# Experts' gate and up projections by Strassen's seven products on 64-column tiles, down blocks spread behind the products

## The reference, cut to what matters

```
D_MODEL = 1024
...
N_EXPERTS = 16
...
D_EXPERT = 2816
...
    xe = h[bidx, idx]
    hid = jax.nn.silu(jnp.einsum('becd,edf->becf', xe, e_gate)) * jnp.einsum('becd,edf->becf', xe, e_up)
    ye = jnp.einsum('becf,efd->becd', hid, e_down) * gate[..., None].astype(h.dtype)
    return jnp.zeros_like(h).at[bidx, idx].add(ye)
```

## Time and profile before

| what | us |
|---|---|
| time, median of 3 runs | 3615.91 (3611.45 to 3624.05) |
| span of the profiled execution | 3612.2 |
| first transpose of the experts' stage | 1489.76 |
| first gate matmul | 1494.90 |
| last down matmul ends, about | 3594.96 |

### The profile page before, as it was taken

The page is one execution under the profiler, slowest core; times in us unless marked ns, Lnnn a source line. Parts: engine busy times, 40 slices in busy tenths (PEclk is TensorE's granted clock), DMA queues, the critical chain, the costliest instruction groups (busy, mean ns, idle before and its releaser), DMA issues.

```text
span 3612.2 us, 83473 instructions
## 1 busy us (share of the span) xinstructions
PE 3408.1 (94%) x37698; PEld 2976.7 (82%) x37698; DVE 1102.5 (31%) x2770; ACT 735.5 (20%) x1815; POOL 385.0 (11%) x536
## 2 busy tenths in 40 slices
PE   7989898898999997499999999999999999999998
PEld 3575767667455544499999999999999999999998
DVE  4566666575344444411111111111111111111113
ACT  3435344343244433000000000000000000000002
POOL 0141514233211000000000000000000100000001
PEclk9999999999999998799999999999999999999999
DMA  8200000000311122697777778787778878777775
GB/s 353 71 5 9 18 10 17 5 20 5 102 32 26 43 77 93 226 362 264 281 269 275 268 274 275 264 288 258 272 276 280 275 267 283 263 281 269 274 264 185
DMA packets 500080, 666.46 MB, mean 185 GB/s; under 512 B 31598, under 2 KB 438406, under 8 KB 496654
## 3 DMA queue, kind: packets, MB, share of 16 engines
q1 hardware_dynamic: 494030, 641.74, 50.5%
q0 software_dynamic: 5520, 19.34, 2.0%
q10 hardware_dynamic: 176, 0.05, 0.0%
HBM read 631.68 MB, written 28.30 MB: 183 GB/s over the span
## 4 chain that ended last, share of the span: by engine, by line
PE 58%; SPq 1%; DMA 0%; DVE 0%; ACT 0%; issue 0%; DVEq 0%
PE banks L2465 38%; PE banks L2477 19%; PE banks L2488 0%; PE banks L2423 0%; DMA e_wd<-in_e_down 0%; SPq L2335 0%; SPq L2339 0%; SPq L2336 0%; SPq L2334 0%; ACT e_wd L2558 0%; PE banks L2447 0%; DVE e_ye L2632 0%; DVE e_wu L2718 0%; DVE e_wu L2661 0%; DVE e_xe L2707 0%
## 5 line engine op out<-in xcount | busy, mean ns | idle before, releaser
L2465 PE MATMUL banks<-e_xT,e_wg 128*128 128x144 f32 x5632 | 747.9, 287 | 1.9 <-DVE e_xT L2598 1.6
L2477 PE MATMUL banks<-e_hid,e_wd 128*128 128x144 f32 x5632 | 748.1, 287 | 0.0
L2465 PE MATMUL banks<-e_xT,e_wu 128*128 128x144 f32 x5632 | 747.6, 287 | 0.0
L2465 PEld LDWEIGHTS banks<-e_xT,e_wg 128*128 128x128 f32 x5632 | 713.8, 191 | 2.4 <-DMA e_wd<-in_e_down 2.3
L2465 PEld LDWEIGHTS banks<-e_xT,e_wu 128*128 128x128 f32 x5632 | 713.8, 191 | 0.0
L2477 PEld LDWEIGHTS banks<-e_hid,e_wd 128*128 128x128 f32 x5632 | 711.1, 191 | 0.0
L2608 DVE TENSOR_TENSOR e_tm<-banks,e_sg 128x144 f32<-128x144 f32 x352 | 108.3, 308 | 1790.3 <-ACT e_sg L2544 1790.3
L2544 ACT ACTIVATE e_sg<-banks 128x144 f32<-128x144 f32 x352 | 102.1, 290 | 1937.6 <-PE banks L2465 1937.6
L606 PE MATMUL banks<-hT_x,wblk 128*128 128x512 f32 (+1 forms) x624 | 212.7, 496 | 0.0
L606 PEld LDWEIGHTS banks<-hT_x,wblk 128*128 128x128 f32 x624 | 102.8, 192 | 100.1 <-issue 98.5
L1398 DVE TENSOR_TENSOR r_TW<-r_TW,banks 128x256 f32<-128x256 f32 (+1 forms) x360 | 129.3, 392 | 78.3 <-PE banks L830 74.1
(11 more groups left out here) (383 smaller groups left out, 3572.0 us busy)
## 6 DMA issues: line engine op xcount, KB each, us to landing
e_wg<-in_e_gate SPq DMA_DIRECT2D x176, 1024.0 KB, 5.2
e_wu<-in_e_up SPq DMA_DIRECT2D x176, 1024.0 KB, 7.5
e_wd<-in_e_down SPq DMA_DIRECT2D x176, 1024.0 KB, 10.2
h_wmod<-in_w_mod SPq DMA_DIRECT2D x24, 1024.0 KB, 15.2
wblk<-in_w_in SPq DMA_DIRECT2D x22, 512.0 KB, 21.5
h_x<-in_x_sample SPq DMA_DIRECT2D x8, 512.0 KB, 6.8
wo<-in_w_out SPq DMA_DIRECT2D x2, 2048.0 KB, 12.0
scratch_ffn<-hT_x SPq DMA_DIRECT2D x8, 512.0 KB, 5.2
```

The lines of the kernel that those rows point to most:

```text
L2465: last = nc.tensor.matmul(bank[6 + b % 2][:, j * TOK:(j + 1) * TOK], w[s][:, k, f], xT[e % 2][:, k, :], start=(k == 0), stop=(k == KD - 1))
L2477: last = nc.tensor.matmul(bank[k // PER_BANK][:, c:c + TOK], wd[s][:, b % DUO, k * P:(k + 1) * P], hid[:, b % 2, :], start=(b == 0 and k % ...
```

## The change

**What is computed.** For a duo, gate (and likewise up) is a product of a 256 x 1024 by a 1024 x 144 matrix. It is cut in two by two: hidden units in halves of 128 (columns 0 to 127 and 128 to 255 of a tile), the contraction in halves of 512, tokens in halves of 72 (`HT`). Instead of eight products of these halves seven are formed, of sums of them, and the four results are mixed from the seven. `mats(n)` is 2 for every duo: gate and up both go this way.

**PE.** `product(n, g, q)` is one of the seven for gate (g = 0) or up (g = 1): four pieces of 128 contraction rows, and for each two matmuls, on weight columns 0 to 63 and 64 to 127 (`CS`), to PSUM partitions 0 to 63 and 64 to 127, with 72 tokens streaming. All seven results of one matrix lie in one bank (4 or 6 for gate, 5 or 7 for up). `down` is cut into units of one 128-column output piece, two matmuls of 64 weight columns with 144 tokens, 16 units a duo; `due` gives each unit its step, one or two behind each of the 14 products of a duo, two duos later, and none for some seven steps at an expert's end. The transposes (`turned`) are now matmuls of 64 columns against the identity, four blocks in a row behind the product with q = 3, all through bank 3.

**DVE.** Per duo: four sums of weight halves of 128x1024 elements (L2710, L2715, L2720, L2725), two duos ahead; the mixing of four operations (L2743 to L2750); two multiplications of 128x288 (L2754, L2762). Per expert: four token sums of 128x288 (L2691 to L2696).

**ACT and SP.** ACT copies the first product out (`first_out`) and takes one sigmoid of 288 per duo. Gate and up of a duo share a tile of 2 MB, four of them (`WG`), free when the duo's products are done (`gu_ps`); `wd` keeps six. In the last expert the norm is done four tokens' tiles at a time, behind duos 8 to 10.

```diff
+    def mats(n):
+        return 2 if True else 1
+    def due(i):
+        e, r = divmod(i, ND * UNITS)
+        return STEPS * (ND * e + 2) + r * (STEPS * (ND - 1) + 8) / (ND * UNITS)
...
+        wgu = [sb(f"wgu{i}", [P, 2, KD, DUO * P]) for i in range(WG)]
+        wd = [sb(f"wd{i}", [P, DUO, D]) for i in range(WD)]
+        wsum = [sb(f"wsum{i}", [P, 3, 2, HALF, P]) for i in range(2)]
...
-        SQUARES = {14: (0, 1), 15: (2, 3), 16: (4, 5), 17: (6, 7)}
-        SCALES = {18: (0, 1), 19: (2, 3), 20: (4, 5), 21: (6, 7)}
+        SQUARES = {8: (0, 1, 2, 3), 9: (4, 5, 6, 7)}
+        SCALES = {9: (0, 1, 2, 3), 10: (4, 5, 6, 7)}
...
+                for n in range(N):
+                    e, j = divmod(n, ND)
+                    f = slice(j * DUO * P, (j + 1) * DUO * P)
+                    if n >= WG:
+                        sp.wait_ge(gu_ps, n - WG + 1)
+                    sp.dma_start(wgu[n % WG][:, 0, :, :], gv[:, e, :, f]).then_inc(g_in[n % WG], 16)
+                    sp.dma_start(wgu[n % WG][:, 1, :, :], uv[:, e, :, f]).then_inc(g_in[n % WG], 16)
+                    if n >= WD:
+                        sp.wait_ge(used, n - WD + 1)
+                    sp.dma_start(wd[n % WD][:, :, :], dv[:, e, j * DUO:(j + 1) * DUO, :]).then_inc(d_in[n % WD], 16)
...
+                    for c in CS:
+                        if c.start < n:
+                            c = slice(c.start, min(c.stop, n))
+                            last = nc.tensor.matmul(bank[b][c, out], src[:, c], K.ident[:, :], start=True, stop=True)
+                    return last
...
+                    s = n % WG
+                    x, xs, ws, w = xT[n // ND % 2], xsum[n // ND % 2], wsum[n % 2], wgu[s][:, g, :, :]
+                    k1, k2, f1, f2 = slice(0, HALF), slice(HALF, KD), slice(0, P), slice(P, 2 * P)
+                    t1, t2 = slice(0, HT), slice(HT, TOK)
+                    a = (w[:, k1, f1], w[:, k2, f1], ws[:, 1, g, :, :], w[:, k1, f2], ws[:, 0, g, :, :],
+                         ws[:, 2, g, :, :], w[:, k2, f2])[q]
+                    b = (x[:, k1, t1], x[:, k2, t1], xs[:, 1, :, :], xs[:, 0, :, :], xs[:, 3, :, :], x[:, k2, t2],
+                         xs[:, 2, :, :])[q]
+                    for k in range(HALF):
+                        for c in CS:
+                            last = nc.tensor.matmul(bank[4 + 2 * (n % 2) + g][c, q * HT:(q + 1) * HT], a[:, k, c], b[:, k, :],
+                                                    start=(k == 0), stop=(k == HALF - 1))
...
+                def down(i):
+                    n, r = divmod(i, UNITS)
+                    e, j = divmod(n, ND)
+                    b, k = divmod(r, KD)
+                    if r == 0:
+                        pe.wait_ge(d_in[n % WD], 16 * (n // WD + 1))
+                        pe.wait_ge(hid_ok, n + 1)
+                        if j == 0 and e:
+                            pe.wait_ge(ya_ok, e)
+                            pe.wait_ge(yv_ok, e)
+                    at = (k % PER_BANK) * TOK
+                    for h, c in enumerate(CS):
+                        last = nc.tensor.matmul(bank[k // PER_BANK][c, at:at + TOK],
+                                                wd[n % WD][:, b, k * P + h * CH:k * P + (h + 1) * CH],
+                                                hid[n % 2][:, b, :], start=(j == 0 and b == 0 and k % PER_BANK == 0),
+                                                stop=(j == ND - 1 and b == DUO - 1), skip_group_check=True)
+                    if r == UNITS - 1:
                         last.then_inc(used, 1)
 
-                def output(e, k):
-
-                    if k == 0:
+                def downs(done, time):
+                    while done < N * UNITS and due(done) <= time:
+                        down(done)
+                        done += 1
+                    return done
```

```diff
+                    if n >= 2:
+                        pe.wait_ge(hid_ok, n - 1)
+                    for q in range(QS):
+                        if q == 2:
+                            pe.wait_ge(wsum_ok, n + 1)
+                        last = product(n, 0, q)
+                        if mats(n) == 2:
+                            done = downs(done, STEPS * n + 2 * q)
+                            last = product(n, 1, q)
+                        else:
+                            for i in range(2 * KD * q // QS, 2 * KD * (q + 1) // QS):
+                                last = up(n, i)
+                        if q == QS - 1:
+                            last.then_inc(gu_ps, 1)
+                        done = downs(done, STEPS * n + 2 * q + 1)
+                        if n and q == 3:
+                            between(*divmod(n - 1, ND))
+                done = downs(done, due(N * UNITS))
...
+                def first_out(n):
+                    act.wait_ge(gu_ps, n + 1)
+                    b, m = 4 + 2 * (n % 2), mats(n)
+                    nc.scalar.activation(first[:, 0:m, :], K.psum[:, b:b + m, 0:HT], ACT.Copy).then_inc(first_ok, 1)
...
+                    dve.wait_ge(xv_ok, e + 1)
+                    V.tensor_tensor(xs[:, 0, :, :], b12, b11, ALU.subtract).then_inc(ts_ok, 1)
+                    V.tensor_tensor(xs[:, 3, :, :], b22, b12, ALU.subtract).then_inc(ts_ok, 1)
+                    dve.wait_ge(ts_ok, 3 * e + 1)
+                    V.tensor_tensor(xs[:, 1, :, :], b22, xs[:, 0, :, :], ALU.subtract).then_inc(ts_ok, 1)
+                    dve.wait_ge(ts_ok, 3 * e + 3)
+                    V.tensor_tensor(xs[:, 2, :, :], b21, xs[:, 1, :, :], ALU.subtract).then_inc(xs_ok, 1)
...
+                def sums_first(n):
+                    a11, a12, a21, a22 = weight_blocks(n)
+                    dve.wait_ge(g_in[n % WG], 32 * (n // WG + 1))
+                    V.tensor_tensor(weight_sum(n, 0), a11, a21, ALU.subtract).then_inc(ws_ok, 1)
+                def sums_second(n):
+                    a11, a12, a21, a22 = weight_blocks(n)
+                    dve.wait_ge(ws_ok, 3 * n + 1)
+                    V.tensor_tensor(a21, a21, a22, ALU.add).then_inc(ws_ok, 1)
+                def sums_third(n):
+                    a11, a12, a21, a22 = weight_blocks(n)
+                    dve.wait_ge(ws_ok, 3 * n + 2)
+                    V.tensor_tensor(weight_sum(n, 1), a21, a11, ALU.subtract).then_inc(ws_ok, 1)
+                def sums_last(n):
+                    a11, a12, a21, a22 = weight_blocks(n)
+                    dve.wait_ge(ws_ok, 3 * n + 3)
+                    V.tensor_tensor(weight_sum(n, 2), a12, weight_sum(n, 1), ALU.subtract).then_inc(wsum_ok, 1)
...
+                    dve.wait_ge(gu_ps, n + 1)
+                    dve.wait_ge(first_ok, n + 1)
+                    if n:
+                        dve.wait_ge(hid_ok, n)
+                    V.tensor_tensor(gu[:, 0:m, 0:4:3, :], first[:, 0:m, :].unsqueeze(2).broadcast_to([P, m, 2, HT]),
+                                    blocks(1, 2), ALU.add).then_inc(mix_ok, 1)
+                    dve.wait_ge(mix_ok, 2 * n + 1)
+                    V.tensor_tensor(mixed[:, 0:m, :, :], gu[:, 0:m, 3:4, :].broadcast_to([P, m, 2, HT]), blocks(3, 2), ALU.add)\
+                     .then_inc(mix_ok, 1)
+                    dve.wait_ge(mix_ok, 2 * n + 2)
+                    V.tensor_tensor(gu[:, 0:m, 1:3, :], mixed[:, 0:m, :, :], blocks(5, 2), ALU.add)
+                    V.tensor_tensor(gu[:, 0:m, 3:4, :], mixed[:, 0:m, 1:2, :], blocks(3, 1), ALU.add).then_inc(gu_ok, 1)
+                def gated(n):
+                    dve.wait_ge(sg_ok, n + 1)
+                    V.tensor_tensor(tm[:, :], gu[:, 0, :, :].rearrange("p a b -> p (a b)"), sg[:, :], ALU.mult).then_inc(tm_ok, 1)
+                def hidden(n):
+                    dve.wait_ge(tm_ok, n + 1)
+                    if n >= 2:
+                        dve.wait_ge(used, n - 1)
+                    raised = (gu[:, 1, :, :].rearrange("p a b -> p (a b)") if mats(n) == 2
+                              else bank[5 + 2 * (n % 2)][:, 0:DUO * TOK])
+                    V.tensor_tensor(hid[n % 2][:, :, :].rearrange("p a b -> p (a b)"), tm[:, :], raised, ALU.mult)\
                      .then_inc(hid_ok, 1)
 
```

373 lines of the change are left out of this document (192 added, 181 removed).

## The result

| kernel | median us | runs | profiled span |
|---|---|---|---|
| before | 3618.01 | 3611.45 to 3624.05 | 3612.2 |
| after | 3655.11 | 3645.40 to 3664.57 | 3662.8 |

Each is the median of four executions; the 3615.91 us given for the kernel before ahead of the prediction are the median of three of its four. The ratio is 1.0102, with a 95% interval of 1.0079 to 1.0124. The forecast was 3508 us, range 3494 to 3582: the time lies outside of it, on the side that had a chance of 0.12, and by none of the rivals named there. The profiled execution, the slowest of the four, lies 158.4 us above the sum of 3504.4; the median of the four lies 147 above the 3508.

The account below looks back on a forecast made before the run. PE's row of matmul passes was taken as the bound: 1502.0 + 1232.0 products + 689.9 down + 57.6 transposes + 3.7 stall + 17.2 + 1.1 + 0.9 = 3504.4; the median lies 3.7 above, 3508 us, range 3494 to 3582.

Parts of the forecast that it names:

- the sum of 3504.4: Whole kernel: forecast span in us, from the first product's end, products, down, transposes, the stop near the end and the tail.
- a chance of 0.12: Whole kernel: the chance given to a time slower than before, from DVE as the bound or weight loads taking turns.
- The failed step: PE in the expert stage: it can start a pass each 31 ns, since a scan stretch showed one each 30.7 ns.
- Weights: Weight transfers in the expert stage: 3 MB per 11.25 us, 280 GB/s, asked for 22 us ahead, so hidden.
- Products: Gate and up on PE: 112 pairs of passes at 62.5 ns, 7.00 us a duo, 148 us saved in 176 duos.
- The pace of 65: Rival for gate and up products: a pair costs 65.1 ns, 51 us more, 3559 us; chance 0.13.
- loads in turn: Rival on PE: weight loads of the two halves wait for each other, 111.4 ns a pair, 4472 us; chance 0.07.
- Seams: Changes between 72 and 144 columns on PE: costed at nothing; as rival 5 to 15 ns each, 3533 to 3582; chance 0.12.
- DVE: Sums, mixing and multiplications in the expert stage: 8.3 us a duo per 11.25 of PE, near 75% busy, so hidden.
- The DVE rival: DVE becomes the bound in the expert stage if its copies are dearer; at 1.5 times 3730 us; chance 0.06.
- Start: Beginning of the expert stage: PE may begin at 1498.9, product 0 ends at 1509.0 instead of 1501.9, 7.1 us lost.
- End: Behind the last product: a stall of 3.7 us on `hid`, 1.1 for scalings, 0.9 for transposes, the rest 17.2 us.

Follow-up runs that it names:

- e1: The changed kernel with gate and up weights loaded for the first four duos only, down weights for the first six, then reused; 3515.79 us, before at 3618.51.
- quarters without transfers: The kernel before with gate, up and down matmuls cut into four 32-column pieces, weights loaded for the first six duos only; 3717.01 us, 4114.57 with transfers.
- e3: The changed kernel without DVE's four weight sums per duo from the third duo on; 3652.7 us, before at 3618.51.
- e4: The changed kernel with each unit of down as one matmul of 128 columns instead of two of 64; 4330.77 us, ratio 1.1969.
- e2: The kernel before with its gate, up and down matmuls cut into two 64-column halves; 3688.27 us, ratio 1.0199.
- e9: The changed kernel with Strassen for gate alone, plus 120 fulfilled waits a duo on PE; 4429.49 us, without later weight transfers 4410.69.
- e7: The changed kernel with Strassen's products for gate alone, up as plain products on 64-column halves; 3582.31 us, ratio 0.9893.

## Why the prediction was wrong, and where it was right

**The failed step** is the sentence "PE must start a pass each 31 ns. In a dense stretch of the scan it started 3258 in 100 us, one each 30.7 ns". The row shows that PE can start passes at that pace, and it does: e1 started one each 38.5 ns including down, and quarters without transfers one each 32 ns. But the row's DMA share is 0.02, and the stage at hand has 0.79. It was proof of the pace, and was read as proof of the supply. The term left at nothing was the fetch of instructions under load: 3662.8 - 3514.1 = 148.7 us, of the 158.4 missed. What happens in it is that packets start 2.5 us later beside the transfers, half of them later than PE can bear. The same error is in "**Weights** ... Hidden": what the transfers cost PE in waits for tiles was rightly nothing, what they cost it in packets was not asked. No rival had it either, so the range of 3494 to 3582 was drawn without the case that came.

The page of before had the two numbers that would have raised the question: 297 instruction packets in the page's queue table, and three times the passes per us in the stage after the change. That would not have given the price.

Two small slips changed nothing: the clock of the earlier trace rows is below 9 in two slices, not three, and the two rivals that are slower than before add up to 0.13, not 0.12.

**What held.** 3514.1 of e1, where supply is free, stands 9.7 above the sum of 3504.4.

- Products: 62.5 ns a pair, as taken. The pace of 65 would have made 51 us, loads in turn 964; both fall.
- Seams between 72 and 144 columns cost nothing, as taken; that rival falls.
- DVE: 1.22 us a sum and 455 ns for 288 elements, both as forecast. Its share of the stage was put near 75% and is 61% (65% in e1, 1237.8 of 1900): the sum had counted short gaps as work. The DVE rival falls, by e3 too. `hid` was forecast 5.7 us after the last product; from ACT's first row to the end of the second multiplication it is 5.0, and the view of waits has a single wait of down on `hid`, 2.5 us, the one at the end.

The rows of after for the sum and for 288 elements:

```profile
L2743 DVE TENSOR_TENSOR e_gu<-e_first,banks 128x288 f32<-128x288 f32 x176 | 80.0, 455 | 762.3 <-ACT e_first L2629 565.3
...
L2725 DVE TENSOR_TENSOR e_wsum<-e_wgu,e_wsum 128x1024 f32<-128x1024 f32 x176 | 215.5, 1224 | 5.5
```

- Start: first product forecast at 1498.9, seen at 1498.51; product 0 forecast to end at 1509.0. Time line of after:

```profile
1498.51 3.06 PE L2508 MATMUL banks<-e_xT,e_wgu 128*64 128x72 f32 x64 [3.73 <-issue]
...
1503.38 2.19 PE L2508 MATMUL banks<-e_xsum,e_wsum 128*64 128x72 f32 x32 [1.81 <-DVE e_wsum L2725]
...
1510.13 0.29 ACT L2629 ACTIVATE e_first<-banks 128x144 f32<-128x144 f32 x1 [18.13 <-PE banks L2508]
```

ACT starts when the first result is there, at 1510.1: 1.1 late. After each idle time PE was slow, 3.06 us for 64 passes and 2.19 for 32, where the same 64 take 2.17 and 32 take 1.17 a few us later; the granted clock from 1498 to 1505 us was 0.62. In e1 the first result was 1.2 us later still:

```profile
1511.30 0.29 ACT L2627 ACTIVATE e_first<-banks 128x144 f32<-128x144 f32 x1 [17.99 <-PE banks L2506]
```

- End: a stop of 3.7 us on `hid` was forecast, then 16 units in 3.92. Time line of after:

```profile
3639.12 5.81 PE L2533 MATMUL banks<-e_hid,e_wd 128*64 128x144 f32 x64 [2.49 <-DVE e_hid L2762]
```

The stop was 2.5, and the units took 5.81, 1.9 more: PE came out of the stop with a slower clock, 0.72 from 3639 to 3645 us against 1.00 from 3630 to 3636. The work behind the last down took 17.9 us (3514.1 - 3496.16 in e1) instead of 19.2. For e1, whose end has the same stop and the same 5.81 us, these terms make 2.3 + 1.9 - 1.2 - 1.3 = 1.7 of the 9.7. The other 8.0 lie between the first result and the last down: six gaps between starts of passes make some 6 of them, two at 1513 and 1518 us, while the first tiles still come in, and four later; some 2 aren't placed.

**What stays open.** No row shows the moment at which PE's queue asks for a packet. That it asks at the same place with and without transfers is argued from the instructions on PE being the same, and that a packet then waits behind weight packets in the DMA engines from e1 and from the piece sizes; what exactly holds it up is not shown. How the 1.4 us between a packet's landing and the next pass comes about is not shown. How idle time grows with the need for packets is known at a few points alone (a need of one each 8.15, 6.0, 5.4, 4.9 and 4.1 us under load); where between 6.0 and 5.4 it begins was not looked for.

## What to carry to other kernels

Cutting a matmul into narrower tiles left PE's own time as it was and multiplied its instructions. Count instructions per us and divide 256 by it: that is the time per packet. Here 2.4 us of it went for the packet and what follows it, and what was left was the delay that it could bear beside large transfers: PE stopped at 4.9 us per packet, hardly at 5.4 with cut transfers, and not at 6.0. The cure that worked best was to cut the transfers (256 KB each, one behind each piece of compute). Using the finer tiles only for part of the work cures the stops too, but gives up part of the saving. A row that proves a pace proves it for the DMA share in its own last columns, and should be quoted with it.

## What the runs showed of the hardware

- PE's instructions come in packets of 16 KB and 256 instructions (568 packets, 9.31 MB in after), each some 1.0 us long. PE is served one packet ahead: in e1 a packet starts within some 0.6 us of PE's step into the one before. A first instruction follows its packet's landing by 1.2 us at least, by 1.4 after a stop.
- Beside 270 GB/s of weight transfers in 1 MB pieces a packet starts 2.5 us later in the median, 4.0 at the 95th percentile; with 256 KB pieces 1.6 and 3.3. Without other traffic a packet each 4.1 us was enough (quarters without transfers).
- A change between 128- and 64-column weights on PE costs 0.35 us there and back around one unit of 144 columns (e4), and some 0.25 us around a transpose (e2), although changes in the number of streamed columns cost nothing (after: a product and a unit in 0.75 us).
- A wait on PE for a semaphore that is long reached costs some 39 ns in a dense row of passes (e9 without transfers against e7, one execution).
